# Wide products in the order high, low, low, high instead of high, low, high, low

## What is computed

```python
D_MODEL, SEQ, DEPTH, D_FF = 2048, 256, 2, 5632

def conv_ffn(h, w_up, conv_w, conv_b, w_down):
    u = h @ w_up
    u = lax.conv_general_dilated(u, conv_w[:, None, :], window_strides=(1,), padding=[(CONV_WIDTH - 1, 0)], ...) + conv_b
    gate, up = jnp.split(u, 2, axis=-1)
    return (jax.nn.silu(gate) * up) @ w_down

def reference(x, mem, ...):
    h = x
    for i in range(DEPTH):
        hn = rmsnorm(h, norm_mix[i])
        if i % N_MIXERS == 0:
            h = h + swa_sink_attention(hn, swa_w_qkv[j], swa_w_o[j], swa_sinks[j])
        else:
            h = h + diff_attention(hn, diff_w_qkv[j], diff_w_o[j], ...)
        mem_n = rmsnorm(mem, norm_mem[i])
        h = h + mem_cross_attention(rmsnorm(h, norm_cross[i]), mem_n, x_w_q[i], x_w_kv[i], x_w_o[i])
        h = h + conv_ffn(rmsnorm(h, norm_ffn[i]), ffn_w_up[i], ffn_conv_w[i], ffn_conv_b[i], ffn_w_down[i])
    return rmsnorm(h, norm_final)
```

## Time and profile before

| | |
|---|---|
| median of three timed runs | 2352.13 us (2351.72 to 2352.29) |
| span of the profiled execution, first to last instruction | 2349.5 us |
| the profiled execution's own time, as far as the profile has it | the span of 2349.5 us; the timed median is 2.6 us above it |
| PE busy | 2332.7 us, 14204 products and 14204 weight loads |
| DVE, ACT busy | 1743.6 us, 1192.2 us |
| mean granted clock of TensorE | 0.999 of 2.4 GHz |

### The profile page before, as it was taken

How to read it: one execution, slowest core, us unless ns; L and a number is a source line. 1 busy time by engine, 2 the same in 40 slices (tenths; PEclk the granted TensorE clock), 3 DMA queues, 4 the chain that set the end, 5 groups by cost and what they waited for, 6 DMA issues and landing times.

```text
span 2349.5 us, 34793 instructions
## 1 busy us (share of the span) xinstructions
PE 2332.7 (99%) x14204; PEld 2059.5 (88%) x14204; DVE 1743.6 (74%) x1988; ACT 1192.2 (51%) x1375; POOL 8.6 (0%) x19
## 2 busy tenths in 40 slices
PE   9999999999999999999999999999999999999998
PEld 8988999888888888888988988899888888888887
DVE  7777777877777778777966877777766677676667
ACT  6656556644444444445544454556544444444444
POOL 1000000000000000000000000000000000000000
PEclk9999999999999999999999999999999999999999
DMA  9554434555555555555554554345555555555552
GB/s 323 179 179 144 150 121 157 201 197 190 186 196 184 189 192 185 193 183 178 186 191 133 184 186 162 121 167 197 197 186 190 193 183 195 185 189 181 195 197 90
DMA packets 234016, 425.03 MB, mean 181 GB/s; under 512 B 6944, under 2 KB 48192, under 8 KB 233792
## 3 DMA queue, kind: packets, MB, share of 16 engines
q1 hardware_dynamic: 232896, 421.55, 53.8%
q0 software_dynamic: 688, 1.97, 0.3%
q10 hardware_dynamic: 336, 0.13, 0.0%
HBM read 421.53 MB, written 2.10 MB: 180 GB/s over the span
## 4 chain that ended last, share of the span: by engine, by line
PE 97%; DVE 2%; ACT 1%; issue 0%; ACTq 0%; POOL 0%; DVEq 0%; POOLq 0%
PE pair L380 34%; PE pair L382 17%; PE pair L351 11%; PE pair L353 10%; PE pair L352 10%; PE pair L403 6%; PE pair L405 3%; DVE wlo L268 1%; PE pair L736 1%; PE pair L724 0%; PE pair L1058 0%; PE pair L714 0%; PE pair L711 0%; PE pair L1055 0%; PE pair L749 0%; PE pair L603 0%
## 5 line engine op out<-in xcount | busy, mean ns | idle before, releaser
L268 DVE TENSOR_TENSOR wlo<-raw,whi 128x2048 fp32r<-128x2048 f32 x394 | 900.7, 2289 | 306.5 <-ACT whi L260 305.9
L260 ACT ACTIVATE whi<-raw 128x2048 fp32r<-128x2048 f32 x394 | 753.4, 1914 | 687.8 <-PE pair L382 403.5
L380 PE MATMUL pair<-xx,whi 128*128 128x512 f32 x2880 | 1001.6, 393 | 1.2
L382 PE MATMUL pair<-xx,wlo 128*128 128x256 f32 x2880 | 802.4, 279 | 0.0
L380 PEld LDWEIGHTS pair<-xx,whi 128*128 128x128 f32 x2880 | 539.3, 187 | 126.5 <-issue 5.2
L382 PEld LDWEIGHTS pair<-xx,wlo 128*128 128x128 f32 x2880 | 542.6, 188 | 0.1
L403 PE MATMUL pair<-xx,whi 128*128 128x512 f32 x640 | 229.4, 402 | 0.0
L380 PE MATMUL pair<-oo,whi 128*128 128x512 f32 x640 | 222.6, 391 | 1.2 <-DVE h L1913 1.2
L382 PE MATMUL pair<-oo,wlo 128*128 128x256 f32 x640 | 179.2, 280 | 0.0
L405 PE MATMUL pair<-xx,wlo 128*128 128x256 f32 x640 | 178.5, 279 | 0.0
L351 PE MATMUL pair<-xx,whi 128*128 128x256 f32 x608 | 174.2, 286 | 3.1 <-DVE xx L281 2.3
(11 more groups left out here) (231 smaller groups left out, 3085.0 us busy)
## 6 DMA issues: line engine op xcount, KB each, us to landing
raw<-in_ffn_w_up SPq DMA_DIRECT2D x176, 1024.0 KB, 5.0
raw<-in_ffn_w_down SPq DMA_DIRECT2D x88, 1024.0 KB, 5.0
raw<-in_diff_w_qkv SPq DMA_DIRECT2D x48, 1024.0 KB, 5.2
raw<-in_swa_w_qkv SPq DMA_DIRECT2D x20, 1024.0 KB, 5.1
raw<-in_x_w_kv SPq DMA_DIRECT2D x16, 1024.0 KB, 9.2
raw<-in_swa_w_o SPq DMA_DIRECT2D x16, 1024.0 KB, 5.1
raw<-in_diff_w_o SPq DMA_DIRECT2D x16, 1024.0 KB, 5.0
raw<-in_x_w_q SPq DMA_DIRECT2D x8, 1024.0 KB, 5.3
```

Source lines behind the costliest of these rows:

```text
L260: act.activation(whi[:, s], raw[:, s], ACT.Copy).then_inc(hi_ready, 1)
L268: dve.tensor_tensor(wlo[:, s], raw[:, s], whi[:, s].bitcast(F32), ALU.subtract)\
L380: pe.matmul(banks[m], whi[:, s, k, w], act2[:, c].rearrange("p a t -> p (a t)"), start=c == 0, stop=False, skip_group_check=True)
L382: ins = pe.matmul(banks[m][:, 0:SEQ], wlo[:, s, k, w], act2[:, c, 0], start=False, stop=last and k == 3, skip_group_check=True)
```

## The change

In both wide functions the chunks are taken two at a time: high product of the even chunk, low product of the even chunk, low product of the odd chunk, high product of the odd chunk. Count, shapes, operands and banks of the products stay as they are. The last product of an accumulation, which carries `stop`, and the last of a unit, which carries `units_used`, are now high ones.

```diff
@@ -375,12 +375,22 @@ wide_unit
             for m in range(4):
                 if m == 2 and added is not None:
                     pe.wait_ge(added, count)
-                for k in range(4):
-                    w, c = slice(m * P, (m + 1) * P), 4 * kq + k
-                    pe.matmul(banks[m], whi[:, s, k, w], act2[:, c].rearrange("p a t -> p (a t)"),
-                              start=c == 0, stop=False, skip_group_check=True)
-                    ins = pe.matmul(banks[m][:, 0:SEQ], wlo[:, s, k, w], act2[:, c, 0], start=False,
-                                    stop=last and k == 3, skip_group_check=True)
+                w = slice(m * P, (m + 1) * P)
+
+                def high(k):
+                    c = 4 * kq + k
+                    return pe.matmul(banks[m], whi[:, s, k, w], act2[:, c].rearrange("p a t -> p (a t)"),
+                                     start=c == 0, stop=last and k == 3, skip_group_check=True)
+
+                def low(k):
+                    return pe.matmul(banks[m][:, 0:SEQ], wlo[:, s, k, w], act2[:, 4 * kq + k, 0], start=False,
+                                     stop=False, skip_group_check=True)
+
+                for k in (0, 2):
+                    high(k)
+                    low(k)
+                    low(k + 1)
+                    ins = high(k + 1)
             return ins
@@ -398,12 +408,23 @@ half_block_unit
             for m in range(2):
-                for k in range(8):
-                    w, c = slice(m * P, (m + 1) * P), 8 * half + k
-                    pe.matmul(dst[:, 512 * m:512 * m + 512], high[:, k, w], xx[:, c].rearrange("p a t -> p (a t)"),
-                              start=c == 0, stop=False, skip_group_check=True)
-                    ins = pe.matmul(dst[:, 512 * m:512 * m + SEQ], low[:, k, w], xx[:, c, 0], start=False,
-                                    stop=c == CH - 1, skip_group_check=True)
+                w = slice(m * P, (m + 1) * P)
...
+                for k in range(0, 8, 2):
+                    high_product(k)
+                    low_product(k)
+                    low_product(k + 1)
+                    ins = high_product(k + 1)
             return ins
```

## The result

The changed kernel takes 2356.26 us (median of 17 runs, 2356.03 to 2357.58) against 2351.86 us before (17 runs, 2351.26 to 2353.03): ratio 1.0019, 95% interval 1.0012 to 1.0025. It is 4.4 us slower. The forecast was 2351.0 us and no change; its rival B, a rhythm, is the right kind of cause, but not in the form that it gave.

The account below looks back on a forecast made before the run. The prediction took PE's rate of issuing products as the bound. Steps 0.0, loads and ends 0 and rhythm -1.1 us gave 2349.5 - 1.1 + 2.6 = 2351.0 us, no change, range 2346.0 to 2361.0 us.

Parts of the forecast that it names:

- rival B: Behind two low products pairs fall into the slow rhythm, 6.6 ns each: half 2365 us, all 2377 us; chance 0.14.
- What bounds the kernel: PE, busy for 2332.7 of 2349.5 us, sets the end by the rate at which it issues products.
- What the change touches: Both wide functions: 8320 products, 1442 us of the span, none added or removed; 2080 low-low and 2080 high-high steps arise.
- The price of each step: In the wide units, low-low 120.0 plus high-high 226.7 ns equals an alternating pair's 346.7 ns; change 0.0 us.
- The bound of 3 ns a four: Rounding of starts could hide up to 3 ns on low-low or high-high steps: 6.2 us either side, zero taken.
- Weight loads: Each load hides behind one product; as many have the short cover of a low product as before; cost zero.
- rival C: Loads no longer hide behind two low products: up to +141 us, 2493 us; chance 0.02.
- Ends of units: At a unit's end a high product comes last: 2 ns later per unit, nobody on PE's path waits; cost zero.
- A second rhythm: 20 of 260 units run at some 353.3 ns a pair; half of this slow rhythm taken as shed, -1.1 us.
- The sum: Steps 0.0, loads and ends 0, rhythm -1.1 us: -1.1 us in all, giving 2351.0 us.
- Rival A: Changing product size costs something, and halving the changes gains: 55 us, 2297 us, if all 13.3 ns are due; chance 0.05.
- The signs of being wrong: Fours under 690 ns (Rival A), at 700 or more (rival B), or low-low steps over 125 ns (rival C).

Follow-up runs that it names:

- more cover for the loads: Kernel before with low products of 320 columns in place of 256: 2472.55 us in the order of the change, 2485.92 us alternating.
- the half loads: Kernel before with weight loads of 64 columns for all but a bank's first high product: 2357.02 us in the change's order, 2322.45 us alternating.
- The cycle begun elsewhere: Kernel before with every four ordered high, high, low, low, so a unit ends on low products: 2356.41 us, ratio 1.0019.
- the run with the first four: Kernel before with only the first four products of every unit ordered high, low, low, high, the other 28 alternating: 2374.18 us, ratio 1.0095.

## Why the prediction was wrong

- *What bounds the kernel*: right. PE's rate sets the end; its waits didn't change, and every microsecond is in its steps.
- *What the change touches*: right, 2080 fours, and each unit of them behaves alike.
- *The price of each step*: this step failed. It took the low-low step at 120.0 ns and the high-high step at 226.7 ns from chains of one width, and concluded from 120.0 + 226.7 = 346.7 that a step between widths has no price. The agreement was a property of one mixture, not proof that prices add. Measured in their new places: high-high 233 ns, high-low 231 to 236, low-low 113 to 116, low-high 112 to 119; a four 696.7 instead of 693.4. The bound of 3 ns a four was nearly right in size (3.3), but it was explained as rounding of the rows, with zero as the value. Rounding doesn't leave that much: 0.01 us over 31 or 39 steps is 0.3 ns a step. The trace of before already held signs against additive prices: 353.3 ns a pair in the earlier trace rows, the 232 ns steps of a disturbed chain in the earlier trace rows, and the alternating steps themselves, 230 and 117 ns in place of 226.7 and 120.0 (0.23 us for H-L in the earlier trace rows), which agree with the chains only in their sum.
- *Weight loads*: rival C fell, a low-low step takes 113 to 116 ns and not over 125, and more cover for the loads didn't help. But that loads have no part in the pace was wrong, as the half loads show.
- *Ends of units*: right. The cycle begun elsewhere, with low products at the end, takes the same time.
- *A second rhythm*: the half shed was all shed, 20 units to none. It returned 1.6 us rather than 2.1, since these units went to 696.7 ns, not to 693.3. The sign that was named for it is none: the mean of the half blocks' high products is 402 ns before, with 14 slow half blocks, and 402 ns after (L415), with none.
- *The sum*: +6.4 and -1.6 us in place of 0.0 and -1.1.
- *Rival A* (a change of width costs, fewer changes gain) fell: halving the changes of width lost time, and with 16 products in a row, two changes a unit in place of 32, the kernel is still 3.3 us slower than before. Nor does what a product costs over columns / 2.4 depend on its columns alone: it is 20.0 ns with 384 beside 512 columns, 13.3 with 256 beside 512, and 10.0 there with loads of half the length. The Trainium skill, page "TensorE: Matmul & The Clock Gate", section "Back-to-back issue gap", gives one isolated gap for each width, columns / 2.4 + 2.5 ns; these runs disagree with it.
- *Rival B* had the right kind of cause and the right sign, but not the event: the new order doesn't spread the old slow rhythm, it has one of its own at 696.7 ns. The old one does spread, as B feared, when only a few products are reordered: the run with the first four costs 22.3 us with a net 205 more units in the slow rhythm, where B put 25.3 us on all 240.
- The range held the time, which is luck more than working: it was wide enough by a bound put down to rounding and by a part of B. The forecast of no change, at 0.74, didn't hold: the kernel is slower, and the interval of the ratio leaves out 1. The signs of being wrong, fours under 690 or at 700 and more, leave the 696.7 ns between them; "L-L at 120 and H-H at 227 ns" was the test that caught it. The measured 0.19% lies just inside what the prediction called no difference, and enough runs told it from zero.

## What to carry to other kernels

When TensorE is bound by its issue of products, the price of a product must be read in the sequence in which it will stand: chains of one width say what a chain of one width costs, and their agreement with one mixture proves nothing for another. Alternating 512 and 256 columns ran at the sum of its parts; every other mixture tried with full loads was 0.4 to 3.3% above it in its most frequent rhythm. When a reordering of products looks free, read the steps of a few units before and after; a partial one (the head of each unit) can be far worse than a full one.

## What the runs showed of the hardware

- Behind a change from 256 to 512 moving columns (fp32r), about five steps are slow (233, 236, 229, 232, 231 ns against 226.7), though nothing is waited for.
- Alternating 512 and 256 columns has two lasting rhythms, 346.7 and 353.3 ns a pair; four products ahead of them moved a net 205 of 260 units into the slower and cost 22 us.
- The chains of 256 and of 512 columns alone run at columns / 2.4 GHz + 13.3 ns (120.0 and 226.7 ns). Weight loads of half the length make it 10.0 ns in the alternating order (680.0 ns a four) and put the other order at 693.3 or 700.0 ns a four. Why, no run here tells.
